# Retention's rotation by a transfer within SBUF and products on GpSimd; the dilated rows of the output projection row by row at the first attention's end

## The chip, the core and the metric

One core of a Trainium2 chip runs the whole program. The metric is the device time of one execution in microseconds (us), of which three runs were taken. Five engines work side by side, each through its own list of instructions in order: TensorE (PE, matmuls and transposes), VectorE (DVE), ScalarE (ACT), GpSimd (POOL) and SyncE (SP, which here issues all transfers). They wait for each other by semaphores: an instruction behind a wait stays behind it even where its own inputs are ready.

## The reference

Four transformer layers on 512 tokens of width 1024: two of a first kind ("first layers"), then two of a second kind, which the change leaves alone. A first layer computes

```python
h = rms_norm(x, attn_norm_w); proj = h @ w_in
mixed = concat([retention_mixer(ret_cols), dsa_mixer(dsa_cols), dilated_mixer(dil_cols)])
x = x + mixed @ w_out
h = rms_norm(x, mlp_norm_w)
x = x + square(relu(h @ w_up)) @ w_down
```

The retention mixer has 4 heads of 64. Its queries and keys are rotated by position, `concat([x1*cos - x2*sin, x2*cos + x1*sin])` with x1 and x2 the two halves of a head's 64 rows; then the masked and decayed scores times the values are summed, each head is normalised over its 64 rows (group norm), weighted and gated with silu(g). The dilated mixer (8 heads) is an attention over three patterns, the DSA mixer (4 heads) an attention over the 128 keys per query that an index score picks.

## The kernel before, in words

Activations lie transposed, features on the 128 partitions and 512 tokens along them. Large products run with fp32 split in two parts: a **tile** is three matmuls of 128x128 by 128x512 (high x high, high x low, low x high) into one PSUM bank of 512 columns. A weight slot is 4 blocks of 128 rows by 512 columns: SyncE loads it (`load_slots`, L251), ScalarE makes the high part (`stream_hi`, L260), GpSimd the low part (`stream_lo`, L270), TensorE uses it (`group_tiles`, L280). A group of 16 or 32 tiles fills four banks, a half of PSUM; attention uses banks 0 to 3, weight groups and the retention banks 4 to 7. With `ready` given, `group_tiles` goes through its rows first, all four banks for each row, and waits for each row of the activations apart; without it each bank is finished in turn.

`Attention` (L800) runs a pipeline over units (a head and 128 queries) in numbered steps. In step i TensorE computes the scores of units i and i+1 (even i; it waits for all masks before unit i), the values of unit i-5 (odd i), the transposes ("turn") of unit i-2, and then calls `beside(i)`. The turn of unit k waits for `p_ready` k+1 and for the copy of turn k-1 out of PSUM. VectorE in step i does the mask of unit i, sums and outputs of finished pairs of heads (SUMS, OUT, LOW: the last writes `hid_lo` and signals `mix_lo`), then its `beside(i)`. ScalarE in step i does the exponential of unit i, the copy of turn i-2, then its `beside(i)`. Each of these lists is executed in order.

In `first_layer` (L1172) the dilated attention has 32 units, 39 steps, and 96 tiles beside it (`dil_pace`, steps 0 to 35: queries of DSA with the gate, `retqk`, `retv`). VectorE meanwhile runs the selection of the DSA mixer in rounds (`take`, a maximum of 8 and a replacement, L1546 and L1547): 8 and 4 before the attention, 36 in it, one per step. The output of the dilated mixer is ready with `mix_lo` 4 in step 38. Then the DSA attention runs, 16 units in 23 steps, and the retention and the output projection's dilated rows stand beside it in `retention(i)`, one function per engine:
- steps 0 to 2: 16 tiles of out_a (the dilated rows of `w_out`, first 512 columns), behind `mix_lo` 4, and VectorE's four additions to x (`add_out`, L1584);
- steps 4 and 5 (ROT): the rotation. TensorE multiplies `retqk` (four blocks) by the matrix `rot_m` (L1288), VectorE multiplies the result by sine (L1596), GpSimd has made the product with cosine (L1210), VectorE adds the two (`ret_rotd`, L1598). The tables come with one transfer (`rtab`, 1536 KB, L1197) into the place of the normed activations, once the tiles of `retv` are through;
- steps 6 to 14 (RET): scores (L1297), decay (L1607) and values (L1306) of retention;
- step 14: VectorE copies the sums (L1612); step 15 (GN): mean (L1312), subtraction (L1617), square (L1416); step 16: variance (L1315), logarithm and exponential on ScalarE for `gn_rstd` (L1419, L1422, each with a table load), weight and gate on VectorE (L1622, L1624); step 17: split (L1425, L1629);
- steps 16 to 22: 16 tiles of out_b (the same rows, last 512 columns).

Then follow the other rows (out_c, out_d), behind `mix_lo` 6 and `ret_lo` 2, and the MLP.

Of the kernel before, what the change touches and what calls it, by code (L numbers as in the profile page):

```python
# [9 lines left out]
ALU = mybir.AluOpType  # L10
ACT = mybir.ActivationFunctionType

P = 128
S = 512
# [24 lines left out]
T_IDENT, T_ONES, T_MEAN, T_ROT, T_LOGC, T_CAUSAL, T_POOL = 0, 128, 256, 384, 512, 1024, 1536  # L39
T_SHARED = 1600  # L40
# [10 lines left out]
def shape_tables():  # L51
# [8 lines left out]
    for m in range(P):  # L60
        if m % HD < HD // 2:
            t[m + HD // 2, T_ROT + m] = -1.0
        else:
            t[m - HD // 2, T_ROT + m] = 1.0

# [12 lines left out]
    r[:, T_SIN:T_SIN + S] = np.sin(ang.astype(np.float64))  # L78
# [30 lines left out]
def build(nc, a, out):  # L109
    ctx = ExitStack()  # L110
    with ctx:
# [45 lines left out]
        for i, off in ((2, region + 16384), (3, region + 32768), (4, region), (5, t_off["h_hi"])):  # L157
# [5 lines left out]
        rot_m = tab[:, T_ROT:T_ROT + P]  # L163
# [12 lines left out]
            "ret_rot ret_cos ret_rotd ret_s ret_p ret_o head_w col_T col_ready "  # L176
# [975 lines left out]

        TOKC = TB * IDX_H
# [18 lines left out]
        def first_layer(block, L):  # L1172
# [8 lines left out]
            out_a, out_b = Pace(16, 0, 3), Pace(16, 16, 7)  # L1181
            ROT, RET, GN = 4, 6, 15
# [4 lines left out]
            def _(sp):  # L1187
# [9 lines left out]
                sg["consts"].by(sp.dma_start(rtab[:], a["rtab"]), 16)  # L1197
# [3 lines left out]
            def _(pool):  # L1201
# [4 lines left out]
                stream_lo(pool, pl.s_mix + 2)  # L1206
                pool.wait_ge(*at("consts", 16 * 3))
                pool.wait_ge(sems["bank_free"], BANKS + HALF * (pl.retqk + 1))
                for j in range(4):
                    sg["ret_cos"].by(pool.tensor_tensor(st_b[j][:], retqk[:, j, :], rtab[:, T_COS:T_COS + S], ALU.mult))  # L1210
                stream_lo(pool, nxt.s0)

            @block.tensor
            def _(pe):
# [61 lines left out]
                dil.tensor(pe, lambda i: dil_pace.emit(i, tiles))  # L1276
                tiles_a = tiles_of(pl.out_a, FEAT, hid_hi, hid_lo, k0=KT)
                tiles_b = tiles_of(pl.out_b, FEAT, hid_hi, hid_lo, k0=KT)

                def retention(i):  # L1280
                    if i == 0:
                        pe.wait_ge(*at("mix_lo", 4))
                    out_a.emit(i, tiles_a)
                    if i == ROT:
                        pe.wait_ge(sems["bank_free"], BANKS + HALF * (pl.out_a + 1))
                    if ROT <= i < ROT + 2:
                        for j in (2 * (i - ROT), 2 * (i - ROT) + 1):
                            sg["ret_rot"].by(pe.matmul(ps[:, 4 + j, :], rot_m, retqk[:, j, :], start=True, stop=True))  # L1288
                    if i == RET:
# [19 lines left out]
                    for j in range(2):  # L1309
                        if i == GN:  # L1310
                            pe.wait_ge(*at("gn_in", j + 1))
                            sg["gn_mean"].by(pe.matmul(ps[:, 4 + j, :], mean_m, gn[j][:], start=True, stop=True))  # L1312
# [30 lines left out]
            def _(act):  # L1343
# [53 lines left out]
                def beside_dil(i):  # L1397
# [5 lines left out]
                    if i == len(dil.units) + 1:  # L1403
# [59 lines left out]
            def _(dve):  # L1463
# [100 lines left out]
                def beside_dil(i):  # L1564
# [10 lines left out]
                    else:  # L1575
                        take(1)
# [10 lines left out]
                def retention(i):  # L1587
                    for m in range(4):
# [679 lines left out]
```

## Time and profile before

| | us |
|---|---|
| three runs | 2449.59, 2449.03, 2444.70 (median 2449.03) |
| profiled execution | 2449.56 |
| its span | 2447.6 |
| TensorE busy | 2387.1 (98%), granted clock 0.993 on average |
| VectorE, ScalarE, GpSimd busy | 1041.8, 954.0, 1027.7 |
| bytes moved | 212.36 MB, 87 GB/s |

The two first layers take the first part of the span: the dilated attention of the first runs from about 129 to 225 us and its DSA attention with the retention from there to about 295 us; the second layer's stand 652.5 us later. Line numbers (L312) are those of the kernel before. In a timeline, a number in brackets is the idle time of the engine before the instruction, and behind the arrow stands what ended it. Matmuls overlap, so the distance between starts, and not the duration, is what one costs. An fp32 matmul that isn't split (the rotation's, the retention's) appears as two records.

### The profile page before, as it was taken

To read this page: it belongs to the slowest core of one execution; us is meant where nothing else is said; L and a number is where in the kernel's file an instruction comes from. 1 tells how busy PE (TensorE), PEld (TensorE's weight loads), DVE (VectorE), ACT (ScalarE), POOL (GpSimd) and SP (SyncE) were. 2 spreads that over 40 slices of the span, in tenths; PEclk is the share of its full clock that TensorE was granted. 3 is DMA by queue.
4 is the path that set the end of the run, shared out by engine and by line. 5 is a ranking of instruction groups with operands and counts; after the bars stand their busy time and mean duration, and the time that the engine had idled before them with its cause. 6 is when DMAs were issued, how large, how long until landed. Compare 5 with 4: busy or idle time off the path is not lost.

```text
span 2447.6 us, 29458 instructions
## 1 busy us (share of the span) xinstructions
PE 2387.1 (98%) x11848; PEld 1911.4 (78%) x11848; DVE 1041.8 (43%) x1922; ACT 954.0 (39%) x1329; POOL 1027.7 (42%) x815
## 2 busy tenths in 40 slices
PE   8999999999999989999999999999999999999997
PEld 6777588888877767888888769788889778888887
DVE  4677641121338766221225455322225767322224
ACT  5344452232443445422335355422124384422223
POOL 4432144444444232444444453444444334444442
PEclk9999999999999999999999999999999999999999
DMA  5212023232232121332323212323332312322331
GB/s 164 76 52 96 31 90 103 88 102 90 83 104 86 38 93 37 101 99 91 103 87 116 86 35 70 94 82 101 103 102 88 104 52 87 103 83 90 103 103 52
DMA packets 138279, 212.36 MB, mean 87 GB/s; under 512 B 7456, under 2 KB 65952, under 8 KB 137888
## 3 DMA queue, kind: packets, MB, share of 16 engines
q1 hardware_dynamic: 138144, 210.48, 26.5%
q8 instruction: 94, 1.54, 0.3%
q14 instruction: 41, 0.34, 0.0%
HBM read 208.36 MB, written 2.10 MB: 86 GB/s over the span
## 4 chain that ended last, share of the span: by engine, by line
PE 53%; DVE 5%; ACT 3%; issue 1%; POOL 1%; DMA 0%; ACTq 0%; SPq 0%; DVEq 0%
PE ps L312 47%; PE ps L337 2%; POOL w_lo L275 1%; PE ps L1825 1%; PE ps L844 1%; PE ps L825 1%; PE ps L867 1%; DVE tmp_both L685 0%; DVE x L690 0%; ACT w_hi L266 0%; DVE h_lo L569 0%; DVE ssum L465 0%; ACT L493 0%; PE ps L486 0%; ACT h_hi L561 0%
## 5 line engine op out<-in xcount | busy, mean ns | idle before, releaser
L275 POOL TENSOR_TENSOR w_lo<-raw,w_hi 128x512 fp32r<-128x512 f32 (+1 forms) x776 | 993.6, 1314 | 1380.1 <-ACT w_hi L266 1379.9
L312 PE MATMUL ps<-h_hi,w_hi 128*128 128x512 f32 x1696 | 682.1, 402 | 10.6 <-POOL w_lo L275 10.6
L312 PE MATMUL ps<-h_hi,w_lo 128*128 128x512 f32 x1696 | 663.5, 391 | 0.0
L312 PE MATMUL ps<-h_lo,w_hi 128*128 128x512 f32 x1696 | 663.1, 391 | 0.0
L266 ACT ACTIVATE w_hi<-raw 128x2048 fp32r<-128x2048 f32 (+2 forms) x196 | 361.4, 1854 | 585.0 <-PE ps L312 455.9
L312 PE MATMUL ps<-hid_hi,w_hi 128*128 128x512 f32 x992 | 391.5, 395 | 4.9 <-DVE hid_lo L938 3.9
L312 PEld LDWEIGHTS ps<-h_hi,w_hi 128*128 128x128 f32 x1696 | 318.6, 188 | 90.9 <-issue 18.4
L312 PE MATMUL ps<-hid_lo,w_hi 128*128 128x512 f32 x992 | 388.3, 391 | 0.0
L312 PE MATMUL ps<-hid_hi,w_lo 128*128 128x512 f32 x992 | 388.3, 391 | 0.0
L312 PEld LDWEIGHTS ps<-h_lo,w_hi 128*128 128x128 f32 x1696 | 318.4, 188 | 70.5 <-issue 5.4
L312 PEld LDWEIGHTS ps<-h_hi,w_lo 128*128 128x128 f32 x1696 | 318.0, 187 | 70.4 <-issue 0.4
L312 PEld LDWEIGHTS ps<-hid_hi,w_hi 128*128 128x128 f32 x992 | 187.1, 189 | 47.3 <-DVE hid_lo L938 4.1
L312 PEld LDWEIGHTS ps<-hid_hi,w_lo 128*128 128x128 f32 x992 | 186.8, 188 | 40.2
L312 PEld LDWEIGHTS ps<-hid_lo,w_hi 128*128 128x128 f32 x992 | 187.1, 189 | 39.7 <-issue 0.5
L1584 DVE TENSOR_TENSOR x<-x,ps 128x512 f32<-128x512 f32 x96 | 65.7, 686 | 296.7 <-PE ps L312 296.7
L1655 DVE SCALAR_TENSOR_TENSOR tmp_both<-ps,rstd 128x512 f32<-128x512 f32 x64 | 44.1, 692 | 246.9 <-PE ps L312 223.6
L789 DVE TENSOR_TENSOR tmp_both<-ps,rstd 128x512 f32<-128x512 f32 x48 | 33.0, 691 | 251.6 <-PE ps L312 251.5
L950 ACT ACTIVATE p<-p,stat 128x128 f32<-128x128 f32 (+3 forms) x128 | 71.8, 561 | 156.5 <-DVE stat L912 156.3
L1968 ACT ACTIVATE tmp_both<-tmp_both 128x512 f32<-128x512 f32 x44 | 27.6, 631 | 233.2 <-DVE tmp_both L789 231.9
L2227 DVE TENSOR_TENSOR acc<-acc,ps 128x512 f32<-128x512 f32 x64 | 44.0, 688 | 111.0 <-PE ps L312 110.9
L906 DVE CUSTOM_DVE_ANT_0 p<-ps,tab 128x128 f32<-128x128 f32 (+3 forms) x104 | 49.3, 474 | 75.1 <-PE ps L832 38.4
L337 PE MATMUL ps<-hid_hi,w_hi 128*128 128x256 f32 x256 | 73.9, 289 | 2.0 <-DVE macc L2129 2.0
(304 smaller groups left out, 2776.2 us busy)
## 6 DMA issues: line engine op xcount, KB each, us to landing
raw<-in_w_up SPq DMA_DIRECT2D x32, 1024.0 KB, 5.5
raw<-in_w_down SPq DMA_DIRECT2D x32, 1024.0 KB, 5.0
raw<-in_ffn_w_gate SPq DMA_DIRECT2D x44, 512.0 KB, 3.9
raw<-in_ffn_w_up SPq DMA_DIRECT2D x44, 512.0 KB, 4.9
raw<-in_w_in SPq DMA_DIRECT2D x20, 1024.0 KB, 5.0
raw<-in_ffn_w_down SPq DMA_DIRECT2D x20, 1024.0 KB, 5.0
raw<-in_w_out SPq DMA_DIRECT2D x8, 1024.0 KB, 5.6
raw<-in_ev_w_in SPq DMA_DIRECT2D x8, 1024.0 KB, 5.2
```

Source lines behind the costliest of these rows:

```text
L266: act.activation(w_hi[slot.buf][:, 0:slot.rows, 0:slot.width], raw[r][:, 0:slot.rows, 0:slot.width], ACT.Copy).then_inc(sems["hi_split"], 1)
L275: pool.tensor_tensor(w_lo[slot.buf][:, k, 0:slot.width], raw[r][:, k, 0:slot.width], w_hi[slot.buf][:, k, 0:slot.width].bitcast(F32), ALU. ...
L312: mm = pe.matmul(o, lh, rh, start=first and q == 0, stop=last and q == 2, skip_group_check=True)
L337: mm = pe.matmul(o, lh, rh, start=first and q == 0, stop=last and q == 2, skip_group_check=True)
L789: sg["bank_free"].by(dve.tensor_tensor(o, src, rstd[:, 0:width], ALU.mult))
L825: mm = pe.matmul(ps[:, e, 0:n], a_q[rows, j, q], a_k[rows, kb, 0:n], start=c == 0, stop=last)
L906: sg["s_masked"].by(dve.tensor_tensor_reduce(out=p_t[i % self.PB][:, 0:w], in0=ps[:, e, 0:w], in1=self.bias(qb), scale=1.0, scalar=TAKEN, ...
L950: sg["p_ready"].by(act.activation(p_t[i % self.PB][:, 0:w], p_t[i % self.PB][:, 0:w], ACT.Exp, bias=sn[:, i:i + 1], scale=SCALE, accum_out ...
L1584: sg["bank_free"].by(dve.tensor_tensor(x[:, b, :], x[:, b, :], ps[:, HALF * st.groups[g].half + m, :], ALU.add))
L1655: sg["bank_free"].by(dve.scalar_tensor_tensor(out=tmp[n % 2][:], in0=ps[:, HALF * st.groups[g].half + m, :], scalar=0.0, in1=rstd[:], op0= ...
L1968: sg["relu_ready"].by(act.activation(tmp[m][:], tmp[m][:], ACT.Silu))
L2227: sg["bank_free"].by(dve.tensor_tensor(acc[:, b, :], acc[:, b, :], src, ALU.add))
```

## The change

Tables: `rot_m` is dropped from the shared table (1600 to 1472 columns), and the sine table carries the sign, minus for the first 32 rows of each head. The rotation: once the tiles of `retv` are through, SyncE loads only sine and cosine (512 KB), then copies `retqk` within SBUF into `swap` with the 32-row halves exchanged, four transfers of 32 partitions by 8 KB, then loads the decay table (1 MB). GpSimd multiplies `retqk` by cosine and `swap` by sine, 128x512 each, four of each, and does so before it splits out_b's weights instead of after. VectorE only adds. The sums stand in steps 1 and 2, the retention starts in step 4 instead of 6, the group norm in step 13 instead of 15, with the mean in banks 6 and 7.

Output projection: out_a goes row by row (`ready`), 12 of its tiles in the last two steps of the dilated attention, the other 4 at the start of the DSA attention; its additions to x stand in steps 1 and 2. out_b runs in steps 12 to 20. VectorE takes two rounds of the selection instead of one in the even steps below 20, and ScalarE computes the gate's silu in step 18 of the dilated attention instead of step 33.

```diff
-    r[:, T_SIN:T_SIN + S] = np.sin(ang.astype(np.float64))
+    sign = np.where(np.arange(P) % HD < HD // 2, -1.0, 1.0)[:, None]
+    r[:, T_SIN:T_SIN + S] = np.sin(ang.astype(np.float64)) * sign
...
+        swap = place("swap", [P, 4, S], where=t_off["h_lo"] + 4 * 2048)
...
-            out_a, out_b = Pace(16, 0, 3), Pace(16, 16, 7)
-            ROT, RET, GN = 4, 6, 15
+            out_b = Pace(16, 12, 9)
+            ROT, RET, GN = 1, 4, 13
...
                 sp.wait_ge(sems["bank_ready"], HALF * (pl.retv + 1))
-                sg["consts"].by(sp.dma_start(rtab[:], a["rtab"]), 16)
+                sg["consts"].by(sp.dma_start(rtab[:, 0:T_DECAY], a["rtab"][:, 0:T_DECAY]), 16)
+                sp.wait_ge(sems["bank_free"], BANKS + HALF * (pl.retqk + 1))
+                for r in range(0, P, HD // 2):
+                    o = r ^ (HD // 2)
+                    sg["ret_swap"].by(sp.dma_start(swap[r:r + HD // 2, :, :], retqk[o:o + HD // 2, :, :]), 16)
+                sg["decay_in"].by(sp.dma_start(rtab[:, T_DECAY:], a["rtab"][:, T_DECAY:]), 16)
                 load_slots(sp, nxt.s0)
...
-                stream_lo(pool, pl.s_mix + 2)
+                stream_lo(pool, pl.s_mix + 1)
                 pool.wait_ge(*at("consts", 16 * 3))
                 pool.wait_ge(sems["bank_free"], BANKS + HALF * (pl.retqk + 1))
                 for j in range(4):
                     sg["ret_cos"].by(pool.tensor_tensor(st_b[j][:], retqk[:, j, :], rtab[:, T_COS:T_COS + S], ALU.mult))
+                pool.wait_ge(*at("ret_swap", 16 * 4))
+                for j in range(4):
+                    sg["ret_sin"].by(pool.tensor_tensor(swap[:, j, :], swap[:, j, :], rtab[:, T_SIN:T_SIN + S], ALU.mult))
                 stream_lo(pool, nxt.s0)
...
-                dil.tensor(pe, lambda i: dil_pace.emit(i, tiles))
-                tiles_a = tiles_of(pl.out_a, FEAT, hid_hi, hid_lo, k0=KT)
+                tiles_a = tiles_of(pl.out_a, FEAT, hid_hi, hid_lo, k0=KT, ready=("mix_lo", base["mix_lo"] + 1 - KT))
+
+                def beside_dil(i):
+                    dil_pace.emit(i, tiles)
+                    if i >= dil.steps() - 2:
+                        some(tiles_a, 6)
+
+                dil.tensor(pe, beside_dil)
...
                 def retention(i):
                     if i == 0:
-                        pe.wait_ge(*at("mix_lo", 4))
-                    out_a.emit(i, tiles_a)
-                    if i == ROT:
+                        rest(tiles_a)
+                    if i == RET:
                         pe.wait_ge(sems["bank_free"], BANKS + HALF * (pl.out_a + 1))
-                    if ROT <= i < ROT + 2:
-                        for j in (2 * (i - ROT), 2 * (i - ROT) + 1):
-                            sg["ret_rot"].by(pe.matmul(ps[:, 4 + j, :], rot_m, retqk[:, j, :], start=True, stop=True))
-                    if i == RET:
                         pe.wait_ge(*at("ret_rotd", 4))
...
-                    if i == len(dil.units) + 1:
+                    if i == 18:
                         act.wait_ge(sems["bank_free"], BANKS + HALF * (pl.dsaq + 1))
                         alink(act, act.activation(gate[:], gate[:], ACT.Silu))
...
-                        take(1)
+                        take(2 if i < 20 and i % 2 == 0 else 1)
...
                 def retention(i):
-                    for m in range(4):
-                        if out_a.step_of(4 * (m + 1)) + 1 == i:
+                    if ROT <= i < ROT + 2:
+                        for m in (2 * (i - ROT), 2 * (i - ROT) + 1):
                             add_out(pl.out_a, m, m)
-                    if i == ROT:
-                        dve.wait_ge(*at("consts", 16 * 3))
-                    if ROT <= i < ROT + 2:
                         for j in (2 * (i - ROT), 2 * (i - ROT) + 1):
-                            dve.wait_ge(*at("ret_rot", j + 1))
-                            link(dve, dve.tensor_tensor(gn[j % 2][:], ps[:, 4 + j, :], rtab[:, T_SIN:T_SIN + S], ALU.mult))
                             dve.wait_ge(*at("ret_cos", j + 1))
-                            sg["ret_rotd"].by(dve.tensor_tensor(retqk[:, j, :], gn[j % 2][:], st_b[j][:], ALU.add))
-                            dve.wait_ge(*at("ret_rotd", j + 1))
+                            dve.wait_ge(*at("ret_sin", j + 1))
+                            sg["ret_rotd"].by(dve.tensor_tensor(retqk[:, j, :], swap[:, j, :], st_b[j][:], ALU.add))
+                    if i == RET:
+                        dve.wait_ge(*at("decay_in", 16))
```

## Rows read from the trace of the kernel before

**Rows 1.** The page's first part: busy time, share of the span and instructions.
```profile
PE 2387.1 (98%) x11848; PEld 1911.4 (78%) x11848; DVE 1041.8 (43%) x1922; ACT 954.0 (39%) x1329; POOL 1027.7 (42%) x815
```
**Rows 2.** Timeline of TensorE, late dilated attention: start, duration in us, engine, line, operation, [idle before].
```profile
213.17 0.52 PE L844 MATMUL ps<-tab,p 128*128 128x128 f32 x3 [0.28 <-issue]
...
216.57 0.52 PE L844 MATMUL ps<-tab,p 128*128 128x128 f32 x3 [1.22 <-ACT p L950]
```
**Rows 3.** Timeline of TensorE at the start of out_a.
```profile
227.74 0.50 PE L312 MATMUL ps<-hid_hi,w_hi 128*128 128x512 f32 x1 [1.93 <-DVE hid_lo L938]
...
233.56 0.39 PE L312 MATMUL ps<-hid_hi,w_hi 128*128 128x512 f32 x1
...
236.28 0.39 PE L312 MATMUL ps<-hid_hi,w_hi 128*128 128x512 f32 x1
```
**Rows 4.** Timeline of TensorE, steps 4 to 7 of the DSA attention.
```profile
242.41 1.88 PE L1288 MATMUL ps<-retqk,tab 128*128 128x512 f32 x4
244.22 0.44 PE L867 MATMUL ps<-pT,dsa_v 128*64 128x128 f32 x4
...
247.06 0.50 PE L825 MATMUL ps<-hid_hi,dsaq_hi 64*128 64x512 f32 x2 [0.32 <-DVE stat L906]
...
248.35 0.52 PE L844 MATMUL ps<-tab,p 128*128 128x128 f32 x3 [0.33 <-ACT pT L963]
251.05 1.13 PE L1297 MATMUL ps<-retqk 64*128 64x512 f32 x4 [2.18 <-DVE retqk L1598]
```
**Rows 5.** Windows: length, busy of PE, PEld, DVE, ACT, POOL; PEclk; DMA share; GB/s.
```profile
227.70:233.00 5.30, 5.26 (x16) 4.19 (x17) 1.43 (x7) 2.82 (x6) 4.56 (x4) 0.68 0.97 395
250.50:257.00 6.50, 5.90 (x29) 2.60 (x29) 4.42 (x11) 2.38 (x6) 1.62 (x1) 0.74 0.49 161
```
**Rows 6.** Timeline of TensorE around the group norm.
```profile
274.65 0.52 PE L844 MATMUL ps<-tab,p 128*128 128x128 f32 x3 [0.97 <-ACT p L950]
...
277.71 1.98 PE L1315 MATMUL ps<-ret_st,tab 128*128 128x512 f32 x4
...
286.96 0.66 PE L852 MATMUL ps<-tab,rb 128*128 128x128 f32 x4 [1.07 <-DVE rb L926]
```
**Rows 7.** Transfers by line: count, size of one, median us from issue to landing.
```profile
raw<-in_w_in SPq DMA_DIRECT2D x12, 512.0 KB, 3.7
...
rtab<-in_rtab SPq DMA_DIRECT2D x2, 1536.0 KB, 6.4
...
raw<-in_w_in SPq DMA_DIRECT2D x4, 256.0 KB, 3.5
```
**Rows 8.** Instructions on the tile ret_st: duration in ns (min/median/max), first and last start.
```profile
L1210 POOL TENSOR_TENSOR ret_st<-retqk,rtab x8: 1294/1302/1306, 233.4 to 889.6; 128x512 f32<-128x512 f32 x8
L1598 DVE TENSOR_TENSOR retqk<-gn,ret_st x8: 691/801/1496, 244.3 to 902.5; 128x512 f32<-128x512 f32 x8
```
**Rows 9.** Timeline of ScalarE around the group norm.
```profile
273.36 0.72 ACT L950 ACTIVATE p<-p,stat 128x512 f32<-128x512 f32 x1 [0.97 <-DVE stat L912]
...
274.08 0.47 ACT L963 ACTIVATE pT<-ps 128x384 f32<-128x384 f32 x1
...
282.80 1.15 ACT L1422 ACTIVATE ret_st<-ret_st 128x512 f32<-128x512 f32 x2
```
**Rows 10.** Timeline of VectorE behind the group norm's last product.
```profile
286.25 0.20 DVE L923 RECIPROCAL stat<-stat 128x8 f32<-128x8 f32 x1
```
**Rows 11.** VectorE's groups by line, whole span: count, busy us, mean ns, idle before.
```profile
L1546 DVE MAX8 top<-sc 128x8 f32<-128x256 f32 (+2 forms) x96 | 53.1, 553 | 0.6
L1547 DVE MATCH_REPLACE8 sc<-top,sc 128x256 f32<-128x256 f32 (+2 forms) x96 | 52.1, 543 | 0.0
```
**Rows 12.** Window over the dilated attention's first half, columns as in rows 5.
```profile
128.00:180.00 52.00, 51.94 (x313) 37.71 (x311) 39.35 (x125) 24.61 (x59) 15.12 (x12) 1.00 0.15 47
```
**Rows 13.** Instructions of line 1405, columns as in rows 8.
```profile
L1405 ACT ACT_TABLE_LOAD  x2: 1283/1283/1283, 221.5 to 874.0; - x2
L1405 ACT ACTIVATE gate<-gate x2: 1057/1058/1058, 222.8 to 875.3; 128x1024 f32<-128x1024 f32 x2
```

More of the change, by code:

```diff
@@ L37 @@
 HALF = 4
-T_IDENT, T_ONES, T_MEAN, T_ROT, T_LOGC, T_CAUSAL, T_POOL = 0, 128, 256, 384, 512, 1024, 1536
-T_SHARED = 1600
+T_IDENT, T_ONES, T_MEAN, T_LOGC, T_CAUSAL, T_POOL = 0, 128, 256, 384, 896, 1408
+T_SHARED = 1472
 T_COS, T_SIN, T_DECAY = 0, 512, 1024
@@ L58, in shape_tables @@
     t[:, T_MEAN:T_MEAN + P] = half / HD
[L60 to L64, printed above, removed]
     dist = q - (np.arange(S)[None] - (S - P))
@@ L162, in build @@
         mean_m = tab[:, T_MEAN:T_MEAN + P]
-        rot_m = tab[:, T_ROT:T_ROT + P]
         p_t = [place(f"p{i}", [P, S], where=t_off[n]) for i, n in enumerate(("sq0", "sq1", "ssum", "p_more"))]
@@ L175, in build @@
             "relu_ready hid_sq hid_hi_done hid_lo_done v_ready q_high q_low kk_high kk_low k_high k_low kv_high dq_high dq_low sel_done lfr_zero f_high f_low idx_relu idx_ready idx_used kv_up kv_out ckv_in ckv_n "
-            "ret_rot ret_cos ret_rotd ret_s ret_p ret_o head_w col_T col_ready "
+            "ret_swap decay_in ret_sin ret_cos ret_rotd ret_s ret_p ret_o head_w col_T col_ready "
             "pool_hi pool_lo gn_in gn_mean gn_c gn_sq gn_var gn_rstd gn_out ret_hi ret_lo mix_hi mix_lo s_ready "
@@ L1311, in retention @@
                             pe.wait_ge(*at("gn_in", j + 1))
-                            sg["gn_mean"].by(pe.matmul(ps[:, 4 + j, :], mean_m, gn[j][:], start=True, stop=True))
+                            sg["gn_mean"].by(pe.matmul(ps[:, 6 + j, :], mean_m, gn[j][:], start=True, stop=True))
                         if i == GN + 1:
@@ L1616, in retention @@
                             dve.wait_ge(*at("gn_mean", j + 1))
-                            sg["gn_c"].by(dve.tensor_tensor(gn[j][:], gn[j][:], ps[:, 4 + j, :], ALU.subtract))
+                            sg["gn_c"].by(dve.tensor_tensor(gn[j][:], gn[j][:], ps[:, 6 + j, :], ALU.subtract))
                     if i == GN + 1:
```

## The prediction

> **What bounds the kernel now.** I read the page first. TensorE is busy for 2387 of 2447.6 us [rows 1], so whatever leaves TensorE, and whatever hole in its work closes, comes off the end; other engines matter only by whom they make wait. So the second view is TensorE's timeline through one first layer, read for the bracketed idle times. Each layer has the same holes (the second repeats them within 0.01 us, 652.5 us later), so all sums are made for one layer and doubled. Five places matter:
> - Late in the dilated attention a turn (transpose) waits 0.28 us and another 1.22 us for ScalarE [rows 2].
> - Between it and the output projection's dilated rows (out_a) TensorE waits 1.93 us for VectorE's `mix_lo` 4 [rows 3].
> - The rotation costs matmuls, and then the first retention score waits 2.18 us for `retqk`, after 0.32 and 0.33 us [rows 4].
> - After both holes the granted clock is down: a mean of 0.68 over 5.3 us and 0.74 over 6.5 us [rows 5]. That is 5.3 x 0.32 = 1.7 and 6.5 x 0.26 = 1.7 us of full-speed work lost each time, stretches at the lower level (1.2 GHz) after TensorE had stood for about 2 us.
> - Around the group norm there are 0.97 and 1.07 us [rows 6].
>
> **What is removed, per layer.** (a) Rotation: four fp32 matmuls, in two pairs. The first pair starts at 242.41 and the next matmul at 244.22, so 1.8 us a pair, 3.6 us [rows 4]. All of it is TensorE time with nothing beside it. (b) Twelve out_a tiles move into the last two steps of the dilated attention. In row order (`ready`) they need only `mix_lo` 1 to 3, which are long there, and by the time row 4 is wanted, 12 tiles later, `mix_lo` 4 is there too. A tile is three matmuls; twelve matmuls lie between 233.56 and 236.28, so 0.68 us a tile [rows 3] and 8.2 us of cover for a hole of 1.93. The hole and its clock fall go: 1.93 + 1.7 = 3.6 us. Weights: `w_lo` of this slot was split long before. (c) The waits at the rotation: 0.32 + 0.33 + 2.18 + 1.7 = 4.5 us [rows 4, 5]. Sum removed: 11.7 us.
>
> **What comes in its place at the rotation.** Count from t = 0, the last tile of `retv`. SyncE issues cosine and sine (512 KB) at once; a load of that size lands after 3.7 us [rows 7]. GpSimd needs 1.30 us per product [rows 8]: four cosine products end at 3.7 + 5.2 = 8.9. The four swap transfers (256 KB each, 1 MB) are issued behind the 512 KB. No transfer within SBUF is in the trace. Bounds: together they are 1.5 MB, like `rtab` before, which lands in 6.4 us, so 6.4; or each takes the 3.5 us of a 256 KB load, one after another, so about 14 [rows 7]. I take the lower, as it is one queue that moved `rtab` as one piece, so the swap is hidden behind the cosines. Decay (1 MB) and the next weight slots queue behind it on SyncE, but are wanted only later. GpSimd also now splits out_b's weights (5 us) after the products rather than before them; they are wanted eight steps later, so nothing.
> Sine products then end at 10.2, 11.5, 12.8, 14.1 if undisturbed. TensorE meanwhile: 12 tiles to 8.2, scores of units 0 and 1 to 8.7, four tiles to 11.5, then only scores 2 and turns 0 and 1, to about 12.4 (before, ten tiles and the rotation stood here). It cannot go on: scores 4 want masks 2 and 3, and these stand on VectorE behind the additions to x and the sums `ret_rotd` of steps 1 and 2, which wait for GpSimd. VectorE: two additions to 11.1, then `ret_rotd`. An operation of VectorE with both inputs in SBUF has taken from 0.69 to 1.50 us beside GpSimd [rows 8], so I let the two take turns: sums 1 and 2 end at 12.2 and 14.2, mask 14.8, additions 16.1, sums 3 and 4 17.3, mask 3 17.9. TensorE stands for 17.9 - 12.4 = 5.5 us; without the taking of turns, 4.1. The Trainium skill (SBUF — State Buffer, "SBUF: two separate sides") calls this an exclusive lock for the whole instruction between GpSimd and a VectorE operation with two SBUF inputs; by it the stall is the 5.5, without it the 4.1, which would be 2.8 us over both layers. I take 5.5. After it the clock falls: 1.7 by rows 5, and since both rows follow shorter holes, up to twice that; I take 1.7. Cost: 7.2 us.
>
> **What comes in at the group norm.** GN moves from step 15 to 13, but there are still 16 units of this attention. VectorE waits in step 14 for `gn_rstd`, with mask 15 queued behind it; ScalarE has exponential 15 and, behind that, the copy of turn 13 queued; and turn 14 on TensorE, step 16, waits for this copy. Before, all masks and exponentials were issued by then. The chain from the start of the variance matmuls: 277.71 to the end of `gn_rstd` at 282.80 + 1.15 is 6.2 us [rows 6, 9]; now exponential 14 comes ahead of it on ScalarE, +0.6; VectorE is through with the norm at 286.25, 2.3 us after [rows 10]; mask 15, exponential 0.72 and copy 0.47 [rows 9] with their handovers about 2.3. Together 11.4. TensorE has in that time the variance 1.7, four out_b tiles 2.7, values 0.6 and a turn 0.5, so 5.5. It stands for 5.9 us, with a clock fall, 1.7. Against this the holes of 0.97 (the same chain in small: turn 13 waits for a copy that stands behind an exponential at 273.36 and copy at 274.08) and 1.07 go, covered by out_b tiles [rows 6, 9]. Cost: 5.9 + 1.7 - 2.0 = 5.6 us, bounds 5 and 8. At the end out_b is through about 0.3 us before `mix_lo` 6: 0.3 us.
>
> **The dilated attention.** Ten of VectorE's rounds of the selection go into steps 0 to 18. One is 0.55 + 0.54 = 1.1 us and a short load between [rows 11], 11 to 12 in all; VectorE is idle for 52 - 39.4 = 12.6 us there [rows 12]. So it just fits in sum, but not in each pair of steps: where two masks, an evacuation and an o_norm meet, scores come late; I put 1.0 us, bounds 0 and 3. The later steps are rid of them: the holes of 0.28 and 1.22 go, 1.5 us [rows 2]. Silu moves to step 18, where ScalarE's copies are wanted two steps on: 1.28 for its table, 1.06, and 1.28 for the exponential's table again [rows 13] make 3.6 us; the slack to turn 18 is about 2.8, so 0.8 us, bounds 0 and 2. Net: 1.5 - 1.0 - 0.8 = -0.3 us. The smaller tables' load at the start and the shorter `tab` are worth nothing: other loads stand ahead.
>
> **The sum, per layer:** +11.7 - 7.2 - 5.6 - 0.3 - 0.3 = -1.7, so 3.4 us slower over both. The profiled execution took 2449.56 us (span 2447.6); it lies 0.5 us above the median of 2449.03. So 2449.56 + 3.4 - 0.5 = 2452.5, say 2452 us.
>
> **Rivals.**
> - **The swap is the bound (slower).** If the transfers need 3.5 us each in turn, they land at t = 14.4 rather than behind the cosines at 8.9, and every later step waits 5.5 us more: 2452 + 11 = 2463. It decides from landing later than 8.9 on. For it: 32 partitions a piece, never seen here; against: the queue otherwise moves 1.5 MB in 6.4 us. The Trainium skill (SBUF — State Buffer, "Can I just issue two DMAs to hit both halves?" and the table of ports above it) says that a transfer on 32 partitions moves about 189 GB/s and that two do not add up; by an estimate from that, 1 MB takes some 5.5 us and lands only 0.5 us after the cosines, 1 us in all. No run shows it yet.
> - **The norm's chain doesn't hold TensorE (faster).** If mask 15 or the copy is not behind the norm, 5.9 + 1.7 us a layer come back: 2452 - 15 = 2437. Against it is the order of the code on VectorE and ScalarE, and that the trace shows the same chain in small (0.97).
> - **Engines overlap better (faster).** No taking of turns (1.4), and VectorE's and ScalarE's extra work fits (1.8): 2452 - 6.4 = 2445.6; some more if a clock fall is spared (1.7 each).
> - **The moved tiles don't fill the hole (slower).** If out_a waits in step 37 for its weights or for `retv`'s last bank, 3.6 us a layer stay: 2459. VectorE is less loaded there than before, so little speaks for it.
>
> **How the numbers follow.** Forecast 2452 (its own range 2446 to 2458, from the bounds above): 0.48. Late swap 0.17; no hold by the norm 0.12; better overlap 0.15; hole not filled 0.06. About 0.2% (4.9 us) is what can be told from no change: below 2444.1 is faster, above 2453.9 slower. Faster: 0.12, 0.07 of the overlap case and 0.02 of the forecast, 0.21. Slower: 0.17, 0.06 and 0.14 of the forecast, 0.37. Same: 0.42. The range leaves out most of the 2437 case and what lies over 2463: 2441 to 2463.
>
> **What would show it.** No idle time before out_a; no matmuls of the rotation; a stall of 4 to 6 us before scores 4 of the second attention, named after VectorE; one of about 6 us before a turn after the variance matmuls, named after ScalarE; each followed by a stretch below full clock; a swap landing before the fourth cosine product ends. If the second stall is missing the forecast is wrong by some 15 us; if the swap lands late, the first is 10 us long.

## The result, and the profile after

The changed kernel takes 2462.31 us (median of 4 runs, 2458.73 to 2464.51) against 2447.76 us of the kernel before: ratio 1.0059, interval 1.0047 to 1.0072, or 14.5 us slower. The forecast was 2452 (3.4 us slower, "no change" as the likeliest sign), the range 2441 to 2463. The time lies inside the range, 0.7 us under its top, and the likeliest sign was wrong.

The profiled execution of the changed kernel took 2458.73 us (span 2456.9), the fastest of its four. The first part of its page stands beside [rows 1]: TensorE has 8.0 us less to do, 97% of the span rather than 98%, and the span is 9.3 us longer. So the time is in holes.

```profile
PE 2379.1 (97%) x11832; PEld 1905.5 (78%) x11832; DVE 1041.8 (42%) x1914; ACT 953.1 (39%) x1329; POOL 1039.0 (42%) x823
```

To see where, I cut the first layer of both kernels at three points that have the same work on each side: the start of the dilated attention, the issue of `rtab` (TensorE is through with `retv`), and the first tile of out_c. Windows (length; busy time of PE, PEld, DVE, ACT, POOL; granted clock; DMA share; GB/s), first of the kernel before, then of the changed one:

```profile
128.93:225.37 96.44, 93.63 (x643) 71.12 (x642) 75.92 (x236) 48.60 (x113) 25.77 (x24) 1.00 0.15 45
225.37:294.70 69.33, 62.13 (x352) 39.05 (x353) 40.30 (x103) 31.12 (x66) 16.26 (x12) 0.95 0.20 69
```
```profile
128.61:226.67 98.06, 93.66 (x642) 71.29 (x642) 77.60 (x236) 49.59 (x115) 25.93 (x24) 1.00 0.14 44
226.67:299.98 73.31, 60.14 (x345) 37.58 (x343) 37.67 (x96) 29.70 (x65) 21.64 (x16) 0.88 0.26 80
```

The dilated attention is 1.62 us longer with the same 93.6 us of TensorE work, so all of it is idle time. The second stage is 3.98 us longer: TensorE stands for 73.31 - 60.14 = 13.17 us rather than 69.33 - 62.13 = 7.20, so 5.97 more, and is busy for 1.99 less. As 3.6 us of rotation matmuls left, the matmuls that stayed take 1.6 us more, which is the clock (mean 0.88 rather than 0.95). Together 5.6 us per layer. The two first layers together show it: the first score of the third layer (the first read of `fq_hi`) comes at 1392.3 in the kernel before and at 1403.8 in the changed one, 11.5 us later. The other 3 us of the 14.5 can't be seen in this profile: its execution is 3.6 us below the median of its kernel, at a mean granted clock (0.991) that the three others have too (0.990 to 0.991), and the one of the kernel before is 1.8 us above its median. From the third layer's first score to the end the changed kernel's profile is even 2.2 us shorter (1053.1 rather than 1055.3 us), with a granted clock of 1.00 rather than 0.98 between 1395 and 1600.

The holes themselves, in TensorE's timeline (start, duration, line, [idle before]). Dilated attention, to be held against [rows 2]:

```profile
136.33 0.30 PE L838 MATMUL ps<-tab,p 128*128 128x128 f32 x1 [0.66 <-ACT pT L957]
168.85 0.50 PE L819 MATMUL ps<-hid_hi,dil_q_hi 64*128 64x512 f32 x2 [0.33 <-DVE stat L900]
176.25 0.63 PE L838 MATMUL ps<-tab,p 128*128 128x128 f32 x4 [0.56 <-ACT p L944]
189.91 0.41 PE L838 MATMUL ps<-tab,p 128*128 128x128 f32 x2 [0.77 <-ACT p L944]
208.03 0.30 PE L838 MATMUL ps<-tab,p 128*128 128x128 f32 x1 [1.18 <-ACT rb L949]
217.98 0.52 PE L838 MATMUL ps<-tab,p 128*128 128x128 f32 x3 [0.47 <-ACT p L944]
```

The first three (and one of 0.28 at 170.09) are new and lie where the selection's rounds were doubled; the one at 189.91 is where silu now stands. Late in the stage 1.65 us are left; the kernel before has 2.63 there, since beside [rows 2] it has two more, at 205.27 and 210.29:

```profile
205.27 0.30 PE L844 MATMUL ps<-tab,p 128*128 128x128 f32 x1 [0.91 <-ACT rb L955]
210.29 0.44 PE L867 MATMUL ps<-pT,dil_v 128*64 128x128 f32 x4 [0.22 <-DVE key L933]
```

Sum: 1.83 early, 0.77 for silu, 1.65 late are 4.25, against 2.63: the 1.62 us of the windows. In the second stage nothing stands before out_a any more [rows 3], the holes of [rows 6] are gone, and three others are there:

```profile
243.21 0.45 PE L838 MATMUL ps<-tab,p 128*128 128x128 f32 x1 [4.11 <-ACT pT L957]
246.70 0.69 PE L819 MATMUL ps<-hid_hi,dsaq_hi 64*128 64x384 f32 x2 [3.04 <-DVE stat L900]
289.09 1.09 PE L838 MATMUL ps<-tab,p 128*128 128x128 f32 x4 [5.81 <-ACT p L944]
```

The granted clock after these two places, and after the place where out_a's hole was (windows as above, answer to [rows 5]):

```profile
243.00:250.00 7.00, 3.75 (x13) 1.80 (x13) 4.52 (x9) 1.97 (x8) 5.66 (x4) 0.50 0.02 3
289.00:295.00 6.00, 5.91 (x31) 4.58 (x32) 1.83 (x4) 2.23 (x4) 0.00 (x0) 0.68 0.01 3
228.00:235.00 7.00, 7.00 (x35) 5.56 (x35) 0.56 (x1) 1.01 (x1) 2.99 (x3) 1.00 1.00 234
```

What the chain behind the first two holes did, by engine: the transfers (count, size of one, median us from issue to landing), SyncE's issues of them, GpSimd's products, VectorE's sums.

```profile
swap<-retqk SPq DMA_DIRECT2D x8, 256.0 KB, 6.6
rtab<-in_rtab SPq DMA_DIRECT2D x2, 1024.0 KB, 9.7
rtab<-in_rtab SPq DMA_DIRECT2D x2, 512.0 KB, 5.5
```
```profile
226.67 0.34 SPq L1193 DMA_DIRECT2D rtab<-in_rtab  x1
227.05 3.50 SPq L1197 DMA_DIRECT2D swap<-retqk  x4
```
```profile
232.01 5.04 POOL L1211 TENSOR_TENSOR ret_st<-retqk,rtab 128x512 f32<-128x512 f32 x4 [9.94 <-DMA rtab<-in_rtab]
237.00 5.86 POOL L1214 TENSOR_TENSOR swap<-swap,rtab 128x512 f32<-128x512 f32 x4
242.82 5.84 POOL L269 TENSOR_TENSOR w_lo<-raw,w_hi 128x512 fp32r<-128x512 f32 x4
```
```profile
238.39 3.34 DVE L1599 TENSOR_TENSOR retqk<-swap,ret_st 128x512 f32<-128x512 f32 x2 [0.76 <-POOL swap L1214]
243.38 2.93 DVE L1599 TENSOR_TENSOR retqk<-swap,ret_st 128x512 f32<-128x512 f32 x2
```

The sine products start without a gap behind the cosine ones: the swapped operand was there in time, though only just. Its last transfer landed at about 236.8 (issued at 229.35, 7.4 us to landing), 0.3 us before the cosine products ended. The table was not in time: 512 KB took 5.5 us. And two sums took 3.34 and 2.93 us, where one alone takes 0.69 [rows 8].

### The profile page after: what moved, and what is told of

Same layout as the page of the kernel before. It is cut to its first block, busy times and chain, and to the rows that moved or that the text cites. A ratio compares the mean times of both kernels' runs of the same rounds, so it can differ in the third digit from the quotient of the medians.

```text
span 2456.9 us, 29436 instructions
## 1 busy us (share of the span) xinstructions
PE 2379.1 (97%) x11832; PEld 1905.5 (78%) x11832; DVE 1041.8 (42%) x1914; ACT 953.1 (39%) x1329; POOL 1039.0 (42%) x823
## 3 DMA queue, kind: packets, MB, share of 16 engines
q8 instruction: 94, 1.54, 0.3%
## 4 chain that ended last, share of the span: by engine, by line
PE 81%; DVE 9%; ACT 4%; issue 2%; POOL 2%; DMA 1%; SPq 0%; ACTq 0%; DVEq 0%
PE ps L306 71%; PE ps L331 2%; PE ps L838 2%; PE ps L861 1%; PE ps L819 1%; POOL w_lo L269 1%; DVE sc L1552 1%; DVE top L1551 1%; DVE p L900 1%; PE ps L1827 1%; PE ps L1259 1%; ACT w_hi L260 1%; PE ps L1302 1%; DVE tmp_both L679 0%; DVE x L684 0%
## 5 line engine op out<-in xcount | busy, mean ns | idle before, releaser
L838 PE MATMUL ps<-tab,p 128*128 128x128 f32 x320 | 64.2, 300 | 33.5 <-ACT p L944 20.2
L838 PEld LDWEIGHTS ps<-tab,p 128*128 128x128 f32 x320 | 35.4, 145 | 62.2 <-ACT p L944 43.4
```

The lines of the kernel that those rows point to most:

```text
L838: mm = pe.transpose(ps[:, 2, kb * P:(kb + 1) * P], p_t[i % self.PB][:, kb * P:(kb + 1) * P], ident)
```

## The experiments

Theory: the 14 us are three things, each a wait or a lateness that TensorE stands for: the norm begun at 13 (mask and exponential of turn 15 behind it), the rotation's end (table, products and sums, the sums slowed by GpSimd), and the selection's doubled rounds with the early silu. Rivals: the swap transfer is the bound, the masks behind the sums are the whole of the second hole, or the moved out_a tiles do it. Each ratio below is against runs of the kernel before on the same chip (medians 2447.1 to 2448.9); where a number of the plan helps, I give the start of the third layer's scores, 1403.8 in the changed kernel and 1392.3 in the one before. Each of these starts is read from a single profile: the changed kernel taken once more has 1405.2, and the start of the first dilated attention lies anywhere from 128.6 to 130.0, so differences of about 1 us in them say nothing.

**The norm back at 15.** `norm_at_15`, the changed kernel with

```
-            out_b = Pace(16, 12, 9)
-            ROT, RET, GN = 1, 4, 13
+            out_b = Pace(16, 16, 7)
+            ROT, RET, GN = 1, 4, 15
```

> The changed kernel with the group norm back in step 15 and out_b back in steps 16 to 22; all else stays changed. Theory (the norm's chain on VectorE and ScalarE holds the copy that turn 14 waits for): the hole of 5.8 us before that turn and the lower clock behind it (about 1.9) go, the small holes of 0.97, 0.35 and 1.07 us come back: 5.3 us a layer, so about 10.6 us faster than the changed kernel, some 4 us over the kernel before. Rival (the second attention is bound by its own latencies, and out_b's tiles are what fills them): the hole only moves, total as the changed kernel, about 14 us over before.

Measured: 2452.45 us, ratio 1.0022 (1.0013 to 1.0031), third layer at 1394.8, so 9 us of the 11.5 are back. The hole of 5.81 is gone and those of the kernel before come again, as in these two of four:

```profile
275.99 0.52 PE L838 MATMUL ps<-tab,p 128*128 128x128 f32 x3 [1.18 <-ACT p L944]
288.30 0.66 PE L846 MATMUL ps<-tab,rb 128*128 128x128 f32 x4 [1.06 <-DVE rb L920]
```

The early norm is the largest single cause. It was a little less than expected, since 0.81 and 1.18 us came where 0.97 had been.

**The selection and silu as before.** `selection_old`, the changed kernel with

```
-                    if i == 18:
+                    if i == len(dil.units) + 1:
...
-                        take(2 if i < 20 and i % 2 == 0 else 1)
+                        take(1)
```

> The changed kernel with one round of the selection per step and silu in step 33 again, as before. Theory (VectorE is over its limit in single pairs of steps, and this costs TensorE): the dilated attention is 1.6 us a layer shorter, 3.3 us in all, about 11 us over the kernel before, and the small idle times of TensorE between 130 and 180 us go. Rival (the extra rounds fit, and the later steps gain what these lose): no change, about 14.5 us over before.

Measured: 2459.54 us, ratio 1.0045 (1.0033 to 1.0058), third layer at 1400.6: 3.2 us back over two layers. The early holes are gone and the late ones are exactly the old ones (0.91, 0.22, 0.28, 1.22). So that part costs about 1.6 us per layer; the size is the profile's, as the interval of the ratio overlaps that of the changed kernel. The rounds and silu were put back together, and no run parts them.

**Only the order of masks and sums.** `sums_behind_mask3`, the changed kernel with the four sums in step 3, behind mask 3:

```
-                        for j in (2 * (i - ROT), 2 * (i - ROT) + 1):
+                    if i == 3:
+                        for j in range(4):
```

> The changed kernel with VectorE's four rotation sums all in step 3, behind mask 3, instead of two each in steps 1 and 2 ahead of masks 2 and 3. Theory (masks 2 and 3 queued behind the sums hold TensorE): scores 4 start some 3 us sooner, and a shorter hole comes before the first retention score; the two together about 4.8 instead of 7.15 us a layer, about 5 us faster than the changed kernel, some 9 to 10 over before. Rival (GpSimd's eight products set the end whatever VectorE's order): the whole hole moves to the first retention score, less than 1 us a layer gained, 13 to 14.5 over before.

Measured: 2463.62 us, ratio 1.0061 (1.0047 to 1.0075): no gain. The hole went from the mask to the operands themselves, and the sums were slower still. Rows of TensorE, VectorE and GpSimd:

```profile
249.18 2.08 PE L1302 MATMUL ps<-retqk 64*128 64x512 f32 x4 [5.42 <-DVE retqk L1600]
242.29 6.75 DVE L1600 TENSOR_TENSOR retqk<-swap,ret_st 128x512 f32<-128x512 f32 x4
242.21 6.28 POOL L269 TENSOR_TENSOR w_lo<-raw,w_hi 128x512 fp32r<-128x512 f32 x4
```

Four sums in 6.75 us, side by side with four products of GpSimd in 6.28. That made the next question: is it GpSimd that holds them?

**The same with GpSimd standing still.** `gpsimd_still`, that kernel with one wait more in GpSimd's stream, ahead of the products for the next part:

```
+                pool.wait_ge(*at("ret_rotd", 4))
                 stream_lo(pool, nxt.s0)
```

> As sums_behind_mask3, and GpSimd waits for the four sums before it splits the next weights, so that it stands still while VectorE adds. Theory (a sum, with both inputs in SBUF, waits for the end of GpSimd's running instruction each time): the four sums take 4 x 0.69 = 2.8 us instead of 6.75, the hole of 5.4 us before the first retention score shrinks to about 1.4; about 8 us faster than sums_behind_mask3, 6 to 7 over the kernel before. Rival (the sums are slow by themselves, or the later split of out_b's weights becomes the wait): no gain, about 14 over before.

Measured: 2456.04 us, ratio 1.0036 (1.0023 to 1.005), 7.6 us below `sums_behind_mask3` by the medians, which are from two chips, and about 6 by the ratios. The four sums take 2.50 us, and the hole before the retention scores is 0.97:

```profile
241.53 2.50 DVE L1601 TENSOR_TENSOR retqk<-swap,ret_st 128x512 f32<-128x512 f32 x4
244.17 2.08 PE L1303 MATMUL ps<-retqk 64*128 64x512 f32 x4 [0.97 <-DVE retqk L1601]
```

With the order alone nothing was gained. With both, the idle times at the rotation (1.34, 0.34, 0.28, 0.97 and 0.17) add up to 3.1 us, where the changed kernel has 7.35. The wait without the reordering of the sums was not tried on the changed kernel.

**No swap.** `no_swap`, the changed kernel without the four transfers and the wait for them; it leaves out the exchange of the halves, so the rotation isn't computed:

```
-                    sg["ret_swap"].by(sp.dma_start(swap[r:r + HD // 2, :, :], retqk[o:o + HD // 2, :, :]), 16)
...
-                pool.wait_ge(*at("ret_swap", 16 * 4))
...
+                    sg["ret_sin"].by(pool.tensor_tensor(swap[:, j, :], retqk[:, j, :], rtab[:, T_SIN:T_SIN + S], ALU.mult))
```

> The changed kernel without the four transfers within SBUF and without the wait for them; the sine products read the queries and keys themselves, so the rotation is not computed as the reference has it. Theory (the swap's traffic behind the table's delays the table, which landed 5.5 us after its issue instead of 3.7): the table lands after about 3.7 us, the cosine products start 1.8 us sooner, and the hole at the rotation is 1.8 us a layer shorter; 3.6 us faster than the changed kernel, about 11 over before. Rival (the table's short rows out of longer ones are slow by themselves): table at 5.5 us, no gain, 14.5 over before.

Measured: 2459.88 us, ratio 1.0048 (1.0035 to 1.006), about 2.7 us below the changed kernel by the ratios, whose intervals overlap (the third layer starts at 1403.9, no sooner, in the one profile). The table lands sooner, the cosine products start sooner, and the hole is 2.96 rather than 4.11, with the 3.0 behind it unchanged:

```profile
rtab<-in_rtab SPq DMA_DIRECT2D x2, 512.0 KB, 4.0
```
```profile
242.33 0.45 PE L838 MATMUL ps<-tab,p 128*128 128x128 f32 x1 [2.96 <-ACT pT L957]
```

So the swap delays the load ahead of it on its queue, and it isn't late itself. The size of the delay varies: in the nine profiles of kernels with the swap the table lands 4.4 to 5.8 us after its issue (5.3 and 5.8 in the changed kernel), in this one after 3.8 and 4.1. How much time in all that costs, isn't settled.

**The row-by-row out_a alone.** `out_a_early_only`, the kernel before with the moved tiles of the change and nothing else (`ready`, `some(tiles_a, 6)` in the last two steps, `rest(tiles_a)` in step 0).

> The kernel before with only one part of the change: out_a row by row, 12 of its tiles in the last two steps of the dilated attention and 4 at the start of the second attention; the rotation by matmuls as before. The hole of 1.93 us and the low clock behind it (1.7) go, and the waits in steps 2 to 5, from which ten tiles are gone, come: about 1.5 us. So some 2 us a layer, 4 in all, faster than before. Rival (nothing fills the first steps, and the rotation waits longer for GpSimd's products): no gain or slower than before.

Measured: 2448.52 us, ratio 1.0002 (0.9993 to 1.0011). The hole of 1.93 is gone and this one has come; the hole before the retention scores stays:

```profile
238.83 0.30 PE L844 MATMUL ps<-tab,p 128*128 128x128 f32 x1 [1.34 <-ACT pT L963]
249.01 2.08 PE L1302 MATMUL ps<-retqk 64*128 64x512 f32 x4 [2.19 <-DVE retqk L1603]
```

Closing a hole here mostly let TensorE run ahead into the next one: from out_a to the first retention score the idle times are 4.17 us (1.34, 0.31, 0.33, 2.19) rather than 4.76 (1.93, 0.32, 0.33, 2.18). The 3.6 us that I booked for it were worth nothing by themselves that the times show.

**All three causes taken out.** `all_three` is `gpsimd_still` with the edits of `norm_at_15` and `selection_old`; `all_three_ret6` is the same with retention's units from turn 6 rather than 4.

> gpsimd_still with the group norm in step 15, out_b in steps 16 to 22, and the selection and silu as before the change: the changed rotation and the early out_a tiles are what is left of the change. If the three causes add up (norm 9.2 us, selection 3.4, sums beside GpSimd 8), it is some 6 us faster than the kernel before. Rival (the freed time is taken by the latencies of the second attention, which now has less to do beside it): within 3 us of before or slower.

> As all_three, with the retention in steps 6 to 14 as before the change instead of 4 to 12, so that scores 4 and 6, two turns and values 0 stand ahead of the wait for the sums. Theory (what is left of the hole at the first retention score is the wait for the sums, and other work fills it): 1 to 2 us a layer faster than all_three. Rival (those steps wait for masks and copies themselves): equal to all_three.

Measured: 2444.77 us, ratio 0.9985 (0.9976 to 0.9993), and 2444.19 us, ratio 0.9986 (0.9977 to 0.9995). The third layer starts at 1387.4. The three steps measured one by one (3.2, 9.0 and 5.6 us at the third layer) add up to 17.8; together they give 16.4. That closes the account to within what two profiles of one kernel differ by, and turns a loss of 14 us into a gain of 3.7. When the units begin doesn't matter. But the gain isn't the rotation's: the next run has it, and more, with the old rotation.

**GpSimd standing still in the kernel before.** `before_gpsimd_still`: that one wait, in the kernel before.

> The kernel before with one wait more: GpSimd begins its products for the next part's streams only when VectorE's four sums of the rotation are done. Theory (the two engines take turns when VectorE adds two operands out of SBUF): the four sums go from 1.5 and 0.9 us each to about 0.7, the hole before the matmuls on retqk (2.18 us) shrinks to about 1.1, some 1 us per layer of 12 is not to be had in more than two layers here, so some 2 us in all: ratio about 0.999. GpSimd's own products come about 4 us later and nobody waits for them. Rival: the sums are as slow as before, because something else holds them, and the ratio is 1.000; or the products that come later are then waited for by the third layer's streams, and the ratio is above 1.001.

Measured: 2443.54 us (11 runs), ratio 0.9978 (0.9969 to 0.9986): 5.2 us faster by one line, where 2 were expected, and no slower than `all_three` (0.9985; the third layer starts at 1387.4 in both). What `all_three` keeps of the change, the moved rotation and the early out_a tiles, therefore shows no gain over that line. The four sums now take 691, 691, 691 and 692 ns [rows 8], and the hole before the scores is 1.15:

```profile
249.16 1.13 PE L1298 MATMUL ps<-retqk 64*128 64x512 f32 x4 [1.15 <-DVE retqk L1599]
```
```profile
250.50:257.00 6.50, 5.98 (x50) 3.15 (x47) 4.77 (x17) 3.23 (x11) 3.63 (x3) 1.00 0.22 60
```

Behind that hole there is a new one of 0.52, so the idle times at the rotation fall from 2.83 to 2.32 us only, 1.0 us over both layers. Most of the gain is the clock: 1.00 in the window that has 0.74 in [rows 5], and in the second layer, too, the fall behind the rotation is gone (1.00 from 902 to 914, where the kernel before has 0.84 and 0.59 up to 908). The fall behind the unchanged hole of 1.93 us, ahead of the new wait, is another matter. In the first layer it is missing (1.00 from 227.70 to 233.00, rather than 0.68), in the second layer of the same execution it is there:

```profile
877.90:883.20 5.30, 5.30 (x18) 4.16 (x17) 1.08 (x5) 2.25 (x6) 5.14 (x5) 0.68 0.96 389
```

So some 1.7 us of this profile's gain (the price of such a fall in the prediction, 5.3 x 0.32) is not due to the wait. The mean granted clock of the eleven executions is 0.994 to 0.998, that of the kernel before in the same comparison 0.993 to 0.995. Why the clock stays up behind one such hole and not behind the next stays open.

**The norm one turn early.** `norm_at_14`: `all_three` with `GN` 14 and `out_b = Pace(16, 14, 9)`.

> all_three with the norm begun one turn earlier, at 14 of the output projection's loop. Theory (the hole is the chain of the norm against the work left in the loop): what turn 15 then waits for is only part of the chain, so that the hole before the norm's matmuls is between the 1.1 us of turn 15's place and the 5.8 of the changed kernel's, the ratio against the kernel before between 0.998 and 1.001. Rival: the norm's wait is as long as in the changed kernel (5.8 us), 9 to 10 us in all are lost, ratio 1.002 or more.

Measured: 2441.32 us, ratio 0.997 (0.996 to 0.9981), the lowest median of the study, though the interval overlaps those of `all_three` and of `before_gpsimd_still`. Neither side of the expectation is right. Of the norm's chain only 0.56 us are left, before turn 15. The profile names nothing for it, but ScalarE's row shows what it is: the copy of turn 14 stands right behind the exponentials of `gn_rstd`, and turn 15 starts 0.1 us after its end:

```profile
280.37 0.58 ACT L957 ACTIVATE pT<-ps 128x512 f32<-128x512 f32 x1
281.05 0.63 PE L838 MATMUL ps<-tab,p 128*128 128x128 f32 x4 [0.56 <-issue]
284.94 0.66 PE L846 MATMUL ps<-tab,rb 128*128 128x128 f32 x4 [1.19 <-DVE rb L920]
```

With `GN` at 14 VectorE waits for `gn_rstd` in step 15, and mask 15, the last one, stands ahead of that wait (272.94, the wait's end 279.98); exponential 15 is through before the logarithm, too. It is the same chain as with 13, one place later, with only a copy queued behind it: the cost of 5.8 us was in the queue behind the wait and not in the chain's length.

**The changed kernel once more.**

> The changed kernel once more, on the chip of the two others. Theory: 14 us above the kernel before, ratio 1.006. Rival: the first comparison's ratio was one chip's, and here it is within 1.003.

Measured: 2462.49 us, ratio 1.0057 (1.0044 to 1.0071); the same holes (3.95, 3.05, 5.80) on another chip.

**Everything but the swap.** `all_but_swap` is the kernel before with the still GpSimd, the row-by-row out_a, rotation by TensorE at turns 2 and 3, units from turn 5, and the norm at 14.

> norm_at_14 with the rotation as in the kernel before: by TensorE's product with rot_m, the sine products on VectorE, the table in one load, no transfer within SBUF; out_a row by row, GpSimd still during the sums, rotation at turns 2 and 3, units from turn 5, norm at 14. Theory (the swap is worth nothing, since it moves work onto engines and a queue that then end last): as fast as norm_at_14 or some us faster, ratio 0.996 to 0.997, by the wait for the rotated operands staying at about 1 us and the clock staying whole at 240 to 260. Rival: the swap is worth the 3.6 us per layer of TensorE's rotation matmuls and VectorE's sine products that it takes away; then this kernel is slower than norm_at_14, ratio 0.999 to 1.000.

Measured: 2443.95 us, ratio 0.9985 (0.9976 to 0.9994), so nearer to the rival: the swap is worth something, about 3.7 us by the two ratios (0.9985 and 0.997, whose intervals overlap) and 4.1 by the third layer's start (1389.5 and 1385.4), where 7.2 us of TensorE work leave. The clock fits with its not being more: in both layers' second stage (226 to 300 and 876 to 952) it is 0.95 and 0.96 here, 0.93 and 0.93 in `norm_at_14`. The comparison isn't clean. Here a mask stands behind two sine products and two sums on VectorE, and TensorE waits for what follows from it, a hole that `norm_at_14` doesn't have, while that one has 1.54 for the operands:

```profile
248.31 0.66 PE L844 MATMUL ps<-tab,p 128*128 128x128 f32 x2 [2.99 <-ACT pT L963]
```

Nor is this kernel faster than `before_gpsimd_still` (0.9978): with the old rotation the early out_a and the norm at 14 show no gain over the one wait.

## Why the prediction was right and wrong

Per layer, what I put down and what the trace of the changed kernel has:

| term | predicted us | measured us |
|---|---|---|
| rotation's matmuls gone | -3.6 | -3.6 (16 matmul instructions fewer in two layers, [rows 1] against the page after; the price is that of [rows 4]) |
| hole before out_a gone | -1.9 | -1.9 |
| old holes at the rotation gone | -2.8 | -2.8 |
| new hole at the rotation | +5.5 | +7.35 (4.11, 3.04, 0.20) |
| old holes at the norm gone | -2.0 | -2.0 |
| new hole at the norm | +5.9 | +5.8 |
| end of out_b, small gaps | +0.3 | -0.4 |
| clock: two falls gone, two come | 0 | +1.6 |
| dilated attention | +0.3 | +1.6 |
| sum | +1.7 | +5.6 |

**What held.** The norm: the chain, its names (ScalarE, a turn behind the variance) and its size, 5.81 against 5.9; `norm_at_15` confirms it as the largest cause. The moved out_a tiles closed their hole, so that rival is out. TensorE ran out of work at the rotation 12.4 us after the issue of the table, as worked out (243.21 - 4.11 - 226.67). The swap landed ahead of the cosine products' end, so it wasn't the bound. But it landed 10.1 us after the table's issue, later than the 8.9 by which I wanted to decide; it stayed hidden since the cosine products were late themselves. (The estimate that I set beside it, 0.5 us after the cosines, is 3.7 + 5.5 - 8.9 = 0.3 when worked out.) Silu took 0.77 against 0.8. Engines took turns: the exclusive lock of the Trainium skill (SBUF — State Buffer, "SBUF: two separate sides") was the right reading, and the runs measure it: four sums in 6.75 us beside GpSimd, 2.50 with GpSimd still. The turns aren't quite whole: four sums and four products side by side took 6.8 us (242.21 to 249.04), where one after another they would take 2.50 + 4.97 = 7.5, as far as GpSimd's rough spans can tell.

**What failed, by step.**
- "A load of that size lands after 3.7 us." It took 5.5. The number was the median of loads most of which have none beside them; here four transfers follow on the same queue in 3.5 us. `no_swap` gives 4.0. I asked only when the swap would land and not what it does to the load in front. The products started 1.6 us later than in the sum (2.1 in the second layer), and that is most of the difference of 7.35 and 5.5.
- "After it the clock falls: 1.7 by rows 5 … up to twice that; I take 1.7." Of the two ends I took the lower, for each of the two new holes. The matmuls of the stage lost 1.6 us more than in the kernel before, where I had put no difference: the two holes are 7 and 6 us where the old ones were 2, and windows of 7.0 and 6.0 us behind them have 0.50 and 0.68.
- "The later steps are rid of them: the holes of 0.28 and 1.22 go." They didn't: 1.65 of 2.63 us stay late, at other turns, as TensorE and ScalarE meet there with or without the selection. And the early part cost 1.83 rather than 1.0. `selection_old` puts 3.2 us on this over both layers, against 0.6 in the sum. This term was a mean over a stretch (12.6 us idle for 11 to 12 us of rounds), and the holes come pair by pair.
- The hole before out_a was booked at 1.93 and a clock fall. By `out_a_early_only` that shows no gain in the kernel before. In the sum it did no harm, I think, only because the new hole was counted from the time at which TensorE would run out of work, with the twelve tiles moved.

Beyond the layers, the medians differ by 3 us more than the profiled executions' plan does. No run settles where these lie. The granted clock is the likely place: in the later comparison the changed kernel's executions have means of 0.987 to 0.991 and those of the kernel before 0.993 to 0.995, but the four executions of the first comparison show no such spread.

The range held the time since it reached to the late swap's 2463, so for a reason that didn't occur: that was luck. What carried the time there was three mis-sized terms that went the same way, the hole at the rotation (+1.85 us a layer), the clock (+1.6) and the dilated attention (+1.3), against 0.7 the other way at the end of out_b, and the 3 us that no run places. The load of the table was costed by a row whose loads mostly stand alone on the queue, the doubled rounds by a mean over a whole stretch. (The chances of the five cases add up to 0.98 rather than 1; nothing hangs on it.)

## What to carry to other kernels

When a wait is moved earlier, list what is queued behind it on its engine: the norm's chain cost 5.8 us at turn 13 and 0.6 at turn 14, since at 13 the last mask, and with it an exponential and a copy, stood behind it. Where VectorE adds two operands out of SBUF and TensorE waits for the sum, let GpSimd stand still for that time, if its own result isn't due: one wait was worth 5 us in the kernel before, and with the sums moved behind mask 3 about 6 in the changed kernel. Try such a line before a rebuilt stage: here it brought as much as the repaired change without the norm's move. A transfer issued behind a load on the same queue isn't free for the load.

## What the runs showed of the hardware that I had not expected

- Four transfers of 256 KB from 32 partitions to 32 others took SyncE 3.50 us to issue, against 0.34 for the load of 512 KB ahead of them, and delayed that load's landing from 3.8 and 4.1 us without them to between 4.4 and 5.8 in nine profiles with them. Without them GpSimd starts 4.2 us after the table's issue rather than 5.3 in the changed kernel (231.10 - 226.94 against 232.01 - 226.67).
- The price of two engines at once: a sum of two SBUF operands takes 0.69 us alone and 1.69 in the mean beside GpSimd's products (6.75 / 4), and those slow from 1.24 (4.97 / 4, in `all_but_swap`) to 1.57 us (6.28 / 4).
- One kernel's executions differ by the granted clock: of fifteen of the kernel before on one chip, that with a mean clock of 0.998 took 2441.09 us and that with 0.993 took 2450.3. Behind the same hole of 1.93 us the clock stayed at 1.00 in one layer and fell to 0.68 in the other, within one execution (`before_gpsimd_still`). A single profile's low stretches are therefore no fixed price.
